# Four slots of weights at four addresses: shifting the rings of a two-layer decoder trunk

## The chip, the cores and the metric

The kernel runs on one core of a Trainium2 chip. The metric is the device time of one execution in microseconds, as the median of several runs; a profile records one execution instruction by instruction, and its times count from the start of its span.

## The reference, cut to what matters

16 learned tokens are put ahead of 256 input tokens (272 in all, width 1024), and two layers follow. Everything is float32.

```python
for l in range(2):
    h = h + 0.5 * rmsnorm(swiglu(rmsnorm(h), ffn_w_in[l, 0], ffn_w_out[l, 0]))
    hn = rmsnorm(h)
    u_pool, q, k, v, gate_pool, gate_attn = split(hn @ w_in[l])      # 1024 x 4096 weights
    y_pool = pool_mixer(u_pool) @ w_pool_proj[l]                      # windows 2, 4, 8, 16
    y_attn = sliding_window_attention(q, k, v, sinks[l]) @ w_attn_proj[l]
    merged = sigmoid(gate_pool) * y_pool + sigmoid(gate_attn) * y_attn
    h = h + rmsnorm(merged @ w_o[l])
    h = h + 0.5 * rmsnorm(swiglu(rmsnorm(h), ffn_w_in[l, 1], ffn_w_out[l, 1]))
return h[:, 16:]
```

`swiglu(x)` is `(silu(x @ w_gate) * (x @ w_up)) @ w_out` with an inner width of 2816.

## The kernel before

Activations are kept with the width in the partitions and the 272 tokens along the columns: eight k rows of 128 for x, 22 for the inner width (hid). Each float32 product is made from three products in the float32r format: the weights are split into a high part (the value rounded to float32r) and a low part (what is left), and so are the activations. `products` (L561 to L565) issues high weights by high x (L563), high weights by low x (L564) and low weights by high x (L565), all into one PSUM bank.

Weights come in units of 256 output columns. A unit of layer l has a number u from 0 to 103, and lies in slot `u % RING` of three rings with RING = 4 slots each: `raw` as it comes from HBM, `w_hi` and `w_lo`. A slot holds KD * UW = 8 * 256 float32 values, 8192 bytes in each partition. SyncE's queue loads a unit into `raw` once the low split of the unit four before it is done; ScalarE makes the high part (L1027) once TensorE has used the slot; VectorE makes the low part from raw and high part (L1347); TensorE waits on `lo_done` and then uses the unit, two tiles of 128 output columns, eight k rows each (`unit`, `unit_tile`). In such a product a block of 128 weight columns is the stationary operand, which a load puts into the array, and the rows of x or hid stream past as the moving operand. In some places two or three units are open at once, and TensorE goes through all their tiles for one k row before it takes the next (`deep_three`, `deep_pair`). In the last FFN output of layer 1 (`end_out`, L815 to L835) the roles are turned round: 128 tokens of hid are stationary, and 512 columns of a weight slot stream (L826 to L828).

Layer 1 leaves out the 16 learned tokens where it can: its products then take 256 columns, from column 16 on. SwiGLU's gate and up go to VectorE (L1535, L1543), ScalarE (silu) and GpSimd (L1968 to L1973); the norms are sums of squares by ScalarE, VectorE, GpSimd and TensorE.

Addresses are the subject of the change. The allocator puts tensors one behind the other in each partition, at multiples of 32 bytes. `raw` begins at byte 16,512, so `raw`, `w_hi` and `w_lo` all begin at 128 modulo 256 (16,512, 49,280 and 82,048), and `h` at 114,816, which is 128 as well. A filler `to_start` puts `x_hi` at START = 64 modulo LINE = 256; the rows of x and hid are padded to a multiple of 256 bytes, so that each k row begins at 64 too. X_SHIFT moves x within its row in layer 1: by 40 and 44 elements (160 and 176 bytes) for the high and low part in three of its four stages, to 224 and 240, and with the first 16 columns left out (64 bytes) to 32 and 48. The rows of o are 1120 bytes long, so its eight k rows begin at eight different places modulo 256.

Of the kernel before, what the change touches and what calls it, by code (L numbers as in the profile page):

```python
# [27 lines left out]
F32R = mybir.dt.float32r  # L28
# [5 lines left out]
P = 128  # L34
# [15 lines left out]
KD = D // P  # L50
KF = FF // P
UW = 2 * P
RING = 4
# [17 lines left out]
ROW = -(-T * 4 // LINE) * LINE // 4  # L71
X_SHIFT = (((0, 0),) * 4, ((0, 0), (40, 44), (40, 44), (40, 44)))
HID_SHIFT = (((0, 0), (0, 0)), ((0, 0), (0, 0)))
O_ROW, Z_ROW = T + 8, T + 4
O_SHIFT = 4

# [100 lines left out]
def trunk(nc, x_columns, norm_columns, norm_g, ffn_w_in, ffn_w_out, w_in, pool_w_grp, w_pool_proj,  # L177
          sinks, w_attn_proj, w_o, geometry, out):
    with ExitStack() as ctx:
        def sb(name, shape, dt=F32):  # L180
            return ctx.enter_context(nc.sbuf_tensor(name, shape, dt))
# [3 lines left out]


        raw = sb("raw", [P, RING, KD * UW])
        w_hi = sb("w_hi", [P, RING, KD * UW], F32R)
        w_lo = sb("w_lo", [P, RING, KD * UW], F32R)
        h = sb("h", [P, KD, T])  # L190
        sb("to_start", [P, ((START - nc.sbuf_base) % LINE + LINE) // 4])
        x_hi_rows = sb("x_hi", [P, KD, ROW], F32R)
# [227 lines left out]
        def hid_of(l, f):  # L420

            return [rows[:, :, at:at + T] for rows, at in zip((hid_hi_rows, hid_lo_rows), HID_SHIFT[l][f])]

# [1674 lines left out]
```

## Time and profile before

| | |
|---|---|
| median of 3 runs | 1173.44 us (1171.82 to 1173.93) |
| the profiled execution | 1172.02 us |
| its span, first to last instruction | 1170.2 us |
| granted TensorE clock | 0.998 of full |
| read from HBM | 195.4 MB |

TensorE's matmul records overlap: one begins before the one ahead of it has ended, so a mean duration of 288 ns is no distance between two matmuls. That distance is read from the start times in the timeline. PE stands for matmuls, PEld for the loads of stationary blocks, DVE for VectorE, ACT for ScalarE, POOL for GpSimd. L563 is line 563 of the kernel.

### The profile page before, as it was taken

How to read it: one execution, taken by the hardware profiler on the slowest of the kernel's cores; microseconds unless marked ns; L12 is line 12 of the kernel's file. 1: busy time of each engine (PE TensorE's matmuls, PEld its weight loads, DVE VectorE, ACT ScalarE, POOL GpSimd, SP SyncE). 2: the span in 40 equal slices, each digit the busy share in tenths (PEclk: the TensorE clock that was granted, in tenths of full speed). 3: DMA queues.
4: the chain of work that ended last, by engine and by line, in shares of the span. 5: the costliest groups of instructions: out<-in, count | busy, mean ns of one | idle time of the engine just before them, and what ended most of it. 6: DMA issues, size and time to landing. Idle time of an engine off the chain costs nothing.

```text
span 1170.2 us, 23880 instructions
## 1 busy us (share of the span) xinstructions
PE 1160.6 (99%) x9269; PEld 1133.2 (97%) x9269; DVE 734.0 (63%) x1145; ACT 554.6 (47%) x818; POOL 430.2 (37%) x486
## 2 busy tenths in 40 slices
PE   9999999999999999999999999999999999999997
PEld 8999999999999999999999999999999999999986
DVE  7655546968566865544586555459676668755542
ACT  7433335637554643333554333355376546543441
POOL 1945500007211286541109645000073122965500
PEclk9999999999999999999999999999999999999999
DMA  8854458372365365535646553573733753654540
GB/s 289 265 180 157 148 176 235 116 233 80 91 178 183 109 207 182 176 122 182 210 131 203 185 165 125 189 227 118 251 92 91 197 164 121 221 198 161 192 168 36
DMA packets 197934, 197.58 MB, mean 169 GB/s; under 512 B 4448, under 2 KB 191200, under 8 KB 197856
## 3 DMA queue, kind: packets, MB, share of 16 engines
q1 hardware_dynamic: 197712, 196.44, 53.3%
q8 instruction: 55, 0.90, 0.3%
q14 instruction: 23, 0.19, 0.1%
q10 hardware_dynamic: 144, 0.05, 0.0%
HBM read 195.43 MB, written 1.05 MB: 168 GB/s over the span
## 4 chain that ended last, share of the span: by engine, by line
PE 92%; issue 3%; DVE 2%; ACT 1%; DMA 0%; POOL 0%; SPq 0%; DVEq 0%; ACTq 0%; POOLq 0%
PE bank L563 27%; PE bank L565 27%; PE bank L564 27%; PE bank L826 2%; PE bank L828 2%; PE bank L827 2%; DVE w_lo L1347 1%; PE bank L915 1%; PE bank L910 1%; PE bank L869 1%; PE bank L599 1%; PE bank L598 1%; PE bank L880 1%; PE bank L626 0%; PE bank L872 0%
## 5 line engine op out<-in xcount | busy, mean ns | idle before, releaser
L563 PE MATMUL bank<-x_hi,w_hi 128*128 128x272 f32 (+1 forms) x1991 | 573.3, 288 | 0.8 <-DVE w_lo L1756 0.7
L565 PE MATMUL bank<-x_hi,w_lo 128*128 128x272 f32 (+1 forms) x1991 | 567.4, 285 | 0.0
L564 PE MATMUL bank<-x_lo,w_hi 128*128 128x272 f32 (+1 forms) x1991 | 566.3, 284 | 0.0
L1027 ACT ACTIVATE w_hi<-raw 128x2048 fp32r<-128x2048 f32 (+3 forms) x201 | 339.1, 1693 | 403.1 <-PE bank L565 383.5
L1347 DVE TENSOR_TENSOR w_lo<-raw,w_hi 128x2048 fp32r<-128x2048 f32 (+3 forms) x203 | 421.4, 2081 | 142.5 <-ACT w_hi L1027 142.2
L563 PEld LDWEIGHTS bank<-x_hi,w_hi 128*128 128x128 f32 x1991 | 374.9, 188 | 2.0 <-issue 1.2
L564 PEld LDWEIGHTS bank<-x_lo,w_hi 128*128 128x128 f32 x1991 | 375.6, 189 | 0.3
L565 PEld LDWEIGHTS bank<-x_hi,w_lo 128*128 128x128 f32 x1991 | 374.9, 188 | 0.0
L1968 POOL TENSOR_TENSOR hid_hi<-silu,up_r 128x272 f32 x88 | 142.1, 1615 | 149.3 <-DVE up_r L1543 143.2
L565 PE MATMUL bank<-hid_hi,w_lo 128*128 128x272 f32 x528 | 151.3, 287 | 0.0
L563 PE MATMUL bank<-hid_hi,w_hi 128*128 128x272 f32 x528 | 151.3, 287 | 0.0
L564 PE MATMUL bank<-hid_lo,w_hi 128*128 128x272 f32 x528 | 151.3, 286 | 0.0
L1543 DVE TENSOR_TENSOR up_r<-bank,r 128x272 f32<-128x272 f32 x88 | 38.3, 439 | 103.6 <-PE bank L565 86.5
L563 PEld LDWEIGHTS bank<-hid_hi,w_hi 128*128 128x128 f32 x528 | 99.5, 188 | 0.0
L564 PEld LDWEIGHTS bank<-hid_lo,w_hi 128*128 128x128 f32 x528 | 99.5, 188 | 0.0
L565 PEld LDWEIGHTS bank<-hid_hi,w_lo 128*128 128x128 f32 x528 | 99.5, 188 | 0.0
L1973 POOL TENSOR_TENSOR hid_lo<-hid_f,hid_hi 128x272 f32 x88 | 87.7, 997 | 20.0 <-POOL hid_f L1970 20.0
L1535 DVE TENSOR_TENSOR gate_r<-bank,r 128x272 f32<-128x272 f32 x85 | 36.5, 438 | 88.0 <-PE bank L565 87.7
L1970 POOL TENSOR_TENSOR hid_f<-silu,up_r 128x272 f32<-128x272 f32 x88 | 84.3, 958 | 0.0
L1957 POOL TENSOR_TENSOR rt<-var,half 128x3 f32<-128x3 f32 x6 | 6.1, 1015 | 159.4 <-DVE var L1393 159.4
L1953 POOL TENSOR_TENSOR acc<-acc,sq 128x272 f32<-128x272 f32 x20 | 22.8, 1139 | 95.5 <-ACT sq L1037 94.4
L2004 POOL TENSOR_TENSOR acc<-s,stats 128x16 f32<-128x16 f32 x64 | 19.0, 296 | 88.0 <-DVE stats L1696 87.7
(219 smaller groups left out, 1323.4 us busy)
## 6 DMA issues: line engine op xcount, KB each, us to landing
raw<-in_ffn_w_in SPq DMA_DIRECT2D x84, 1024.0 KB, 5.1
raw<-in_w_in SPq DMA_DIRECT2D x24, 1024.0 KB, 5.6
raw<-in_ffn_w_out SPq DMA_DIRECT2D x24, 768.0 KB, 4.2
raw<-in_ffn_w_out SPq DMA_DIRECT2D x24, 640.0 KB, 3.9
raw<-in_ffn_w_out SPq DMA_DIRECT2D x10, 1024.0 KB, 5.0
raw<-in_w_in SPq DMA_DIRECT2D x16, 512.0 KB, 5.4
raw<-in_w_attn_proj SPq DMA_DIRECT2D x32, 256.0 KB, 4.5
raw<-in_w_o SPq DMA_DIRECT2D x8, 1024.0 KB, 5.5
```

What stands on the lines that cost most here:

```text
L563: pe.matmul(ps[:, t0:T], w[0], a_hi[:, t0:T], start=start, stop=False)
L564: pe.matmul(ps[:, t0:T], w[0], a_lo[:, t0:T], start=False, stop=False)
L565: return pe.matmul(ps[:, t0:T], w[1], a_hi[:, t0:T], start=False, stop=stop)
L826: pe.matmul(ps[:, :], hid_hi[:, k, cols], w[0], start=k == 0, stop=False)
L827: pe.matmul(ps[:, :], hid_hi[:, k, cols], w[1], start=False, stop=False)
L1027: last = act.activation(hi, w, ACT.Copy)
L1347: last = dve.tensor_tensor(lo, w, hi.bitcast(F32), ALU.subtract)
L1535: dve.tensor_tensor(gate_r[:, j, :], bank[4 * (unit // 2 % 2) + j if banks is None else banks[j]][:, 0:T], r[:, :], ALU.mult).then_inc(til ...
L1543: dve.tensor_tensor(up_r[:, j, :], bank[banks[j]][:, 0:T], r[:, :], ALU.mult).then_inc(tile_read, 1)
L1968: pool.tensor_tensor(hid_hi[:, ds(i * 2 + j, 1), :].rearrange("p o t -> p (o t)"), silu[:, j, :], up_r[:, j, :], ALU.mult).then_inc(hid_hi ...
L1970: pool.tensor_tensor(hid_f[:, j, :], silu[:, j, :], up_r[:, j, :], ALU.mult).then_inc(hf_ready, 1)
L1973: pool.tensor_tensor(hid_lo[:, ds(i * 2 + j, 1), :].rearrange("p o t -> p (o t)"), hid_f[:, j, :], hid_hi[:, ds(i * 2 + j, 1), :].rearrang ...
```

## The change

The ring of high weights is allocated with 8 more elements (32 bytes) in each slot, the ring of low weights with 16 more (64 bytes). Everything that uses them sees a view of the first 2048 elements of each slot, as before.

```diff
@@ -71,6 +71,7 @@
 ROW = -(-T * 4 // LINE) * LINE // 4
 X_SHIFT = (((0, 0),) * 4, ((0, 0), (40, 44), (40, 44), (40, 44)))
 HID_SHIFT = (((0, 0), (0, 0)), ((0, 0), (0, 0)))
+HI_STEP, LO_STEP = 8, 16
 O_ROW, Z_ROW = T + 8, T + 4
 O_SHIFT = 4
 
@@ -185,8 +186,8 @@
 
 
         raw = sb("raw", [P, RING, KD * UW])
-        w_hi = sb("w_hi", [P, RING, KD * UW], F32R)
-        w_lo = sb("w_lo", [P, RING, KD * UW], F32R)
+        w_hi = sb("w_hi", [P, RING, KD * UW + HI_STEP], F32R)[:, :, 0:KD * UW]
+        w_lo = sb("w_lo", [P, RING, KD * UW + LO_STEP], F32R)[:, :, 0:KD * UW]
         h = sb("h", [P, KD, T])
         sb("to_start", [P, ((START - nc.sbuf_base) % LINE + LINE) // 4])
         x_hi_rows = sb("x_hi", [P, KD, ROW], F32R)
```

## Rows read from the trace of the kernel before

**Rows 1.** The page's table of engines: busy us (share of the span), instructions.
```profile
PE 1160.6 (99%) x9269; PEld 1133.2 (97%) x9269; DVE 734.0 (63%) x1145; ACT 554.6 (47%) x818; POOL 430.2 (37%) x486
```

**Rows 2.** The waits of TensorE, the longest: us in total, times, longest.
```profile
PE bank L1004 <- DVE r L1339: 1.2, 1, 1.2
```

**Rows 3.** Groups of matmuls by shape: count, busy us, mean ns.
```profile
L563 PE MATMUL bank<-x_hi,w_hi 128*128 128x272 f32 x1401 | 405.0, 289 | 0.8 <-DVE w_lo L1756 0.7
L563 PE MATMUL bank<-x_hi,w_hi 128*128 128x256 f32 x590 | 168.3, 285 | 0.0
L563 PE MATMUL bank<-hid_hi,w_hi 128*128 128x272 f32 x528 | 151.3, 287 | 0.0
L826 PE MATMUL bank<-w_hi,hid_hi 128*128 128x512 f32 x88 | 34.6, 394 | 0.0
```

**Rows 4.** Timeline of layer 0, first FFN: start us, duration us, instruction.
```profile
59.73 0.28 PE L563 MATMUL bank<-x_hi,w_hi 128*128 128x272 f32 x1
...
60.22 0.28 PE L564 MATMUL bank<-x_lo,w_hi 128*128 128x272 f32 x1
60.22 0.19 PEld L565 LDWEIGHTS bank<-x_hi,w_lo 128*128 128x128 f32 x1
...
66.39 0.28 PE L563 MATMUL bank<-x_hi,w_hi 128*128 128x272 f32 x1
```

**Rows 5.** Busy by stretch: PE, PEld, DVE, ACT, POOL, granted clock, DMA.
```profile
50.00:60.00 10.00, 10.00 (x84) 10.00 (x83) 5.85 (x5) 3.67 (x4) 9.12 (x8) 1.00 0.51 156
160.00:170.00 10.00, 10.00 (x84) 10.00 (x83) 4.81 (x3) 3.03 (x3) 0.00 (x0) 1.00 0.58 187
```

**Rows 6.** Timeline: o in layer 0, shifted x in layer 1, 53 starts apart.
```profile
344.81 0.29 PE L565 MATMUL bank<-o_hi,w_lo 128*128 128x272 f32 x1
...
351.44 0.29 PE L564 MATMUL bank<-o_lo,w_hi 128*128 128x272 f32 x1
...
832.75 0.29 PE L564 MATMUL bank<-x_lo,w_hi 128*128 128x272 f32 x1
...
839.40 0.29 PE L563 MATMUL bank<-x_hi,w_hi 128*128 128x272 f32 x1
```

**Rows 7.** Last product: timeline, 52 starts apart; durations ns min/median/max of L828.
```profile
1129.63 0.39 PE L828 MATMUL bank<-w_hi,hid_lo 128*128 128x512 f32 x1
...
1141.41 0.39 PE L826 MATMUL bank<-w_hi,hid_hi 128*128 128x512 f32 x1
...
L828 PE MATMUL bank<-w_hi,hid_lo x88: 388/389/398, 1102.5 to 1163.6; 128*128 128x512 f32 x88
```

**Rows 8.** Loads beside short matmuls in the timeline; durations ns min/median/max.
```profile
207.02 0.19 PEld L599 LDWEIGHTS bank<-x_hi,w_lo 128*128 128x128 f32 x1
...
207.46 0.19 PEld L599 LDWEIGHTS bank<-x_hi,w_lo 128*128 128x128 f32 x1
...
L563 PEld LDWEIGHTS bank<-x_hi,w_hi x1991: 186/188/193, 5.8 to 1101.6; 128*128 128x128 f32 x200
L564 PEld LDWEIGHTS bank<-hid_lo,w_hi x528: 187/188/189, 137.8 to 791.2; 128*128 128x128 f32 x176
```

**Rows 9.** Timeline, 256 columns: ordinary units (57 starts), two units in turn (56).
```profile
951.79 0.28 PE L564 MATMUL bank<-x_lo,w_hi 128*128 128x256 f32 x1
...
958.45 0.28 PE L563 MATMUL bank<-x_hi,w_hi 128*128 128x256 f32 x1
...
1009.73 0.28 PE L565 MATMUL bank<-x_hi,w_lo 128*128 128x256 f32 x1
...
1016.45 0.28 PE L565 MATMUL bank<-x_hi,w_lo 128*128 128x256 f32 x1
```

**Rows 10.** Splits of a full slot by shape: count, busy us, mean ns, idle before.
```profile
L1027 ACT ACTIVATE w_hi<-raw 128x2048 fp32r<-128x2048 f32 x131 | 250.7, 1916 | 269.7 <-PE bank L565 250.3 <-PE bank L828 9.8 <-DMA raw<-in_ffn_w_in 9.3
L1347 DVE TENSOR_TENSOR w_lo<-raw,w_hi 128x2048 fp32r<-128x2048 f32 x133 | 315.8, 2376 | 47.7 <-ACT w_hi L1027 47.5
```

**Rows 11.** The chain that ended last, in order of time: one of its six splits.
```profile
387.49 2.44 DVE w_lo L1347
```

## The prediction, made before the changed kernel ran

> **What bounds the kernel now.** I began with the table of engines: TensorE is busy for 1160.6 of the 1170.2 us, VectorE for 734.0 and ScalarE for 554.6 [rows 1]. The list of waits then says how little TensorE waits for the engines that fill the two rings: 1.2 us for anything at the longest [rows 2], and 0.7 us for a low split [rows 3]. So the time is, to within one per cent, the sum of the distances between the starts of consecutive matmuls. The groups by shape give the counts: products with 272 columns on x and on hid (1401 + 528 per line, three lines, so 5787), 590 per line on x with 256 columns (1770), and 88 per line with 512 columns, where the weights are the moving operand (264) [rows 3]. Their "mean ns of one" is no pace, since matmuls overlap; the pace comes from start times in the timeline. In the first layer 54 starts take 66.39 - 59.73 = 6.66 us, 123.3 ns each [rows 4]; on hid, from 160 to 170 us, as many matmuls fall into 10 us as on x [rows 5]. 272 columns at the granted clock (full, that is 2.4 GHz [rows 5]) are 113.3 ns, so each product carries 10.0 ns more. The change can act on the time almost only through those 10 ns.
>
> **What the change does to addresses.** A slot holds 8192 bytes, a multiple of 256. All four slots of both rings therefore start at byte 128 modulo 256 today, and so does every 128-column block in them (they lie 512 bytes apart). Afterwards the high slots start at 128, 160, 192, 224. The ring of low weights is moved on by the 128 bytes that the high ring gained, so its slots start at 0, 64, 128, 192: slot 0 of the low weights changes too, and only slot 0 of the high ones and slot 2 of the low ones keep their place. h moves from 128 to 0; x_hi and all that lies after it moves by exactly 256, because the filler ahead of x_hi rounds it off. raw stays. No instruction, wait, transfer or byte moved is added or removed. The change does what its description says, so that is no rival here.
>
> **Step 1, the moving operand.** That a start address can set the pace is in this trace. In layer 1 the copy of x is shifted, so that with all 272 columns its high and low parts start at 224 and 240; 53 starts then take 839.40 - 832.75 = 6.65 us, 125.47 ns each, 2.14 ns above the 123.33 at 64 [rows 6]. The o operand, whose eight k rows start at eight residues, runs at (351.44 - 344.81) / 53 = 125.1 ns [rows 6]. These are changes of the moving operand with the weights always at 128. The change moves it in one place: the last output product, where the weights stream. It now runs at (1141.41 - 1129.63) / 52 = 226.5 ns for 512 columns [rows 7]. Its price is between 264 x -4 ns = -1.1 us and 264 x 9 ns = +2.4 us: 4 ns is about twice the 2.14 ns of a 272-column product, for twice the columns; 9 ns is the longest duration of one of its lines above the median, 398 against 389 [rows 7]. I take 4 ns for half the slots, 132 x 4 = +0.5 us.
>
> **Step 2, the stationary operand.** This is where nearly all uses of the two rings lie, and the trace has only one residue of it. What speaks for no effect: the load of the next block starts together with the matmul before it (both at 60.22), and where matmuls are short, loads follow each other at (207.46 - 207.02) / 4 = 110 ns [rows 4, 8]. Against 123.3 ns that leaves a load 13 ns of room in every product, and its own duration hardly moves: 187 to 189 ns on all 528 of a line on hid, 186 to 193 on x [rows 8]. A load that takes a few ns more from 160 than from 128 has that room. What speaks against: in layer 1 the same shifted x with 256 columns runs at (1016.45 - 1009.73) / 57 = 117.9 ns in ordinary units, and at (958.45 - 951.79) / 56 = 118.9 where two units take turns on one k [rows 9]. All residues are the same in both; what differs is the order of weight blocks and banks. So something beside the moving operand's start enters. The two bounds for this step are those of the rivals below, -14 and +14 us; I take 0, since the nearest row, the load on hid, shows neither a wait nor a stretched load.
> The page "TensorE: Matmul & The Clock Gate" of the Trainium skill, Part 2, says that TensorE reads its two operands through two independent ports, so that a load takes nothing from the running matmul. By that rule step 2 is 0. The same page, Part 1, gives a warm pace of columns / 2.4 GHz plus about 2.5 ns, that would be 115.8 ns; the trace disagrees with 123.3. By its figure, as an estimate, 7.5 ns on each of 5787 products (43 us) is a cost that the page has no reason for, and a reader who believes that it is a clash of operands would expect this change to move it. No term of my sum uses it.
>
> **Step 3, writers and readers.** The four slots may have been meant to keep ScalarE's and VectorE's writes away from TensorE's reads. There is nothing to gain: in two stretches of 10 us, with GpSimd idle or busy for 9.12 us, ScalarE for 3.03 or 3.67 and VectorE for 4.81 or 5.85, as many matmuls (84) fall into each [rows 5]. Price 0. The splits themselves, 1916 ns on ScalarE and 2376 ns on VectorE for a full slot [rows 10], are hidden behind TensorE, for which the high splits of full slots waited 250.3 us. Cover is missing in one place per layer: three low splits, up to 2.44 us long, lie on the chain that ended last in layer 0, in the normalisation before the second FFN, and three in layer 1 [rows 11]. Should the new starts change a split by a tenth (0.24 us), six of them are 1.4 us either way; VectorE's reads of h at residue 0 are in the same bound. I take 0. The transfers into raw wait for the low split and land in unchanged slots: 0.
>
> **The sum.** 1170.2 + 0.5 + 0 + 0 = 1170.7 us of span; the profiled execution took 1172.0, so 1.8 us lie around the span, and the median of the three runs, 1173.4, is 1.4 above that execution. 1170.7 + 1.8 + 1.4 = 1173.9; forecast 1174 us. A measurement of this kernel can tell some 0.2% (2.3 us) from no change.
>
> **Rival 1, slower: loads and streams fall out of step.** Suppose the pace depends on the distance between the moving start and the weight block. Then 64 against 128 is today's pair for 5691 products (5787 less the 96 at 224/240), and it has the lowest excess that the trace shows for any pair: 10.0 ns, against 12.1 at 224/240 and 11.8 on o [rows 4, 6]. The change takes the high weights of slots 1 and 3 to another distance by an odd multiple of 32 bytes. If those slots run like the shifted x, half of 5787 products pay 2.14 ns, 6.2 us; half of 1770 pay the 1.0 ns between the two paces with 256 columns [rows 9], 0.9 us; with the 0.5 of step 1 that is 7.6 us, so 1181. If all four slots pay, since the low ones move as well, it is 12.4 + 1.8 + 0.5 = 14.7, so 1188. It decides from a mean pace above 123.8 ns in layer 0 (0.4 ns x 5787 = 2.3 us). For it: the shifted x and the two paces with 256 columns [rows 6, 9]. Against: the unstretched loads and their 13 ns of room.
>
> **Rival 2, faster: the new distances fit better.** By the same mechanism, but today's pair isn't the best one. Half the slots gaining as much as the shifted x loses give -6.2 - 0.9 us, so 1166 to 1167; all slots, and every product at 121.2 ns, give about 1160. Ten ns of excess leave room for it, and no row has a lower one for 272 columns, which is against it. With 256 columns the present excess is 11.2 ns (117.9 - 106.7), above the 10.0 at 272, so there at least a better distance exists.
>
> **How the numbers follow.** No effect through the loads, 0.38, 1174 (1172 to 1175.5 with the bounds of steps 1 and 3). Rival 1, 0.35, 1177 to 1188, most of it about 1181. Rival 2, 0.27, 1160 to 1170, most of it about 1167. Both signs hold much of the chance, since step 2 has no row of its own: the trace shows one residue. For 8 in 10 I leave out the case of all slots on both sides: 1164 to 1185. The likeliest case alone has 1172 to 1176. Chances: faster 0.27, same 0.38, slower 0.35.
>
> **What would show each step.** The pace in the first layer's FFN, start to start over one unit of each slot: 123.3 in all four if step 2 holds. A pattern that repeats every fourth unit, with slots 1 and 3 off, is the distance between the operands; a pace that is off by the same in all units would point at something else. The last product: 226.5 ns in the slots at 128, more in the others if step 1 holds. Durations of loads (188 ns) above 193 would say that a load is stretched. The mean of the full splits, 1916 and 2376 ns, tests step 3. The prediction is wrong if any slot shows another pace on x or hid.

## The result, and the profile after

The changed kernel takes 1185.49 us (median of 4 runs, 1185.28 to 1185.72) against 1172.8 us (4 runs, 1171.82 to 1173.93) of the kernel before, run beside it. The ratio is 1.0107, with a 95% interval of 1.0095 to 1.0118: slower by some 1%, about 13 us. The profiled execution took 1185.55 us with a span of 1183.8 us; the span is 13.6 us longer than that of before. The granted clock is 0.998 in both.

The kernel after, the page's table of engines (busy us, share of the span, instructions), answers to [rows 1]:

```profile
PE 1174.6 (99%) x9269; PEld 1146.0 (97%) x9269; DVE 731.7 (62%) x1145; ACT 555.3 (47%) x818; POOL 429.4 (36%) x486
```

Every count of instructions is the same. TensorE is busy for 14.0 us more, VectorE for 2.3 us less, ScalarE for 0.7 more. The list of TensorE's waits (us in total, times, longest) answers to [rows 2], and hasn't changed:

```profile
PE bank L1005 <- DVE r L1340: 1.2, 1, 1.2
...
PE bank L564 <- DVE w_lo L1757: 0.6, 1, 0.6
```

So no engine makes TensorE wait longer; its matmuls themselves stand further apart. (Every line of the kernel has moved by one: L564 to L566 are the three products here, L827 to L829 those of the last output.) The timeline shows it best. These are the first matmuls of five units in a row in layer 0's first FFN, in slots 0, 1, 2, 3 and 0 again, 48 matmuls from one to the next (start us, duration us, instruction):

```profile
79.86 0.28 PE L564 MATMUL bank<-x_hi,w_hi 128*128 128x272 f32 x1
...
85.89 0.28 PE L564 MATMUL bank<-x_hi,w_hi 128*128 128x272 f32 x1
...
91.87 0.29 PE L564 MATMUL bank<-x_hi,w_hi 128*128 128x272 f32 x1
...
97.91 0.29 PE L564 MATMUL bank<-x_hi,w_hi 128*128 128x272 f32 x1
...
103.99 0.28 PE L564 MATMUL bank<-x_hi,w_hi 128*128 128x272 f32 x1
```

The units take 6.03, 5.98, 6.04 and 6.08 us, which divided by 48 is 125.6, 124.6, 125.8 and 126.7 ns a matmul. Before, it was 123.3 in every slot [rows 4]. No slot kept its pace, and the four differ. From here on "the pace of a slot" is this number; read from two starts given to 0.01 us, it can be off by 0.1 to 0.2 ns. In the changed kernel the means over all such units of layer 0's first FFN are 125.6, 124.5, 125.9 and 126.6, and each slot repeats its own in layer 0's second FFN and in layer 1's first. The last product answers to [rows 7]: two starts 52 matmuls apart lie 12.07 us apart, 232.1 ns each, against 226.5 before.

```profile
1144.72 0.39 PE L827 MATMUL bank<-w_hi,hid_hi 128*128 128x512 f32 x1
...
1156.79 0.40 PE L828 MATMUL bank<-w_lo,hid_hi 128*128 128x512 f32 x1
```

Adding up the distances between consecutive starts in the whole trace, kind by kind, gives the account of the 13.6 us. Distances above 150 ns (250 ns with 512 columns), where TensorE turns to other work or waits, aren't in the rows of the table, so the counts lie a little below those of the instructions:

| products | count | ns before | ns after | us |
|---|---|---|---|---|
| x, 272 columns | 4157 | 123.48 | 125.65 | +9.0 |
| hid, 272 columns | 1584 | 123.34 | 125.70 | +3.7 |
| last output, 512 columns | 259 | 227.36 | 232.21 | +1.3 |
| x, 256 columns | 1742 | 118.07 | 117.97 | -0.2 |

All that is left, the long distances included, changes by -0.2 us together.

Loads, writers and readers hardly moved (VectorE's split is 22 ns shorter). The durations of the loads (ns, shortest/median/longest) answer to [rows 8], and the two splits (count, busy us, mean ns, idle before) to [rows 10]:

```profile
L565 PEld LDWEIGHTS bank<-hid_lo,w_hi x528: 187/188/189, 140.1 to 803.7; 128*128 128x128 f32 x176
L564 PEld LDWEIGHTS bank<-x_hi,w_hi x1991: 186/188/193, 5.8 to 1113.9; 128*128 128x128 f32 x200
```

```profile
L1028 ACT ACTIVATE w_hi<-raw 128x2048 fp32r<-128x2048 f32 x131 | 251.1, 1919 | 275.3 <-PE bank L566 260.3 <-PE bank L829 10.2 <-DMA raw<-in_ffn_w_in 4.4
...
L1348 DVE TENSOR_TENSOR w_lo<-raw,w_hi 128x2048 fp32r<-128x2048 f32 x133 | 312.9, 2354 | 50.5 <-ACT w_hi L1028 50.4
```

A load is recorded with some 188 ns from the new addresses too, and yet the products that use the loaded blocks stand further apart. That is the reading to take from this pair of views: a duration of a load that hasn't changed doesn't say that the pair of load and matmul costs the same.

### The profile page after: what moved, and what is told of

The parts are those of the page before. It is cut to its first block, busy times and chain, and to the rows that moved or that the text cites. A ratio compares the mean times of both kernels' runs of the same rounds, so it can differ in the third digit from the quotient of the medians.

```text
span 1183.8 us, 23880 instructions
## 1 busy us (share of the span) xinstructions
PE 1174.6 (99%) x9269; PEld 1146.0 (97%) x9269; DVE 731.7 (62%) x1145; ACT 555.3 (47%) x818; POOL 429.4 (36%) x486
## 4 chain that ended last, share of the span: by engine, by line
PE 97%; DVE 1%; ACT 0%; DMA 0%; SPq 0%; issue 0%; POOL 0%; DVEq 0%; ACTq 0%
PE bank L564 28%; PE bank L566 28%; PE bank L565 28%; PE bank L827 2%; PE bank L829 2%; PE bank L828 2%; PE bank L916 1%; PE bank L911 1%; PE bank L715 1%; PE bank L599 1%; PE bank L600 1%; PE bank L627 1%; PE bank L870 1%; DVE w_lo L1348 1%; PE bank L881 0%; PE bank L873 0%
## 5 line engine op out<-in xcount | busy, mean ns | idle before, releaser
L564 PE MATMUL bank<-x_hi,w_hi 128*128 128x272 f32 (+1 forms) x1991 | 573.9, 288 | 0.8 <-DVE w_lo L1757 0.6
L566 PE MATMUL bank<-x_hi,w_lo 128*128 128x272 f32 (+1 forms) x1991 | 569.7, 286 | 0.0
L564 PEld LDWEIGHTS bank<-x_hi,w_hi 128*128 128x128 f32 x1991 | 374.8, 188 | 2.0 <-issue 1.2
L566 PEld LDWEIGHTS bank<-x_hi,w_lo 128*128 128x128 f32 x1991 | 374.6, 188 | 0.0
L566 PE MATMUL bank<-hid_hi,w_lo 128*128 128x272 f32 x528 | 152.1, 288 | 0.0
L564 PE MATMUL bank<-hid_hi,w_hi 128*128 128x272 f32 x528 | 152.0, 288 | 0.0
L564 PEld LDWEIGHTS bank<-hid_hi,w_hi 128*128 128x128 f32 x528 | 99.3, 188 | 0.0
L566 PEld LDWEIGHTS bank<-hid_hi,w_lo 128*128 128x128 f32 x528 | 99.3, 188 | 0.0
```

Source lines behind the costliest of these rows:

```text
L564: pe.matmul(ps[:, t0:T], w[0], a_hi[:, t0:T], start=start, stop=False)
L566: return pe.matmul(ps[:, t0:T], w[1], a_hi[:, t0:T], start=False, stop=stop)
```

## The experiments

Every kernel here is the one before with the edit shown, and all compute the whole result. A kernel with a single time below ran once, so differences of 1 to 3 us between two such times say nothing; the verdicts rest on the pace by slot in the 272-column units, read over 48 matmuls at a time. Within one FFN it repeats within 0.3 ns from unit to unit of a slot, with three exceptions: slot 1 of experiment 8 runs at 125.1 to 126.6, slot 1 of experiment 6 once at 124.4 instead of 126.7, and slot 1 of the changed kernel once at 125.0 instead of 124.5. In experiments 2, 3 and 6 to 10 the filler ahead of x_hi is also shortened or taken out to make room; x_hi begins at START modulo 256 all the same. All places are bytes modulo 256. "Distance" is the start of x less the start of the weight block. In the kernel before, high and low weights lie at 128 and x and hid at 64: distance 192 everywhere.

**1. All slots alike, the low ring on its own.** The change does two things: it makes slots differ, and it moves the two rings against each other. This kernel does the second alone.

```diff
+        sb("pad_lo", [P, 32])
         w_lo = sb("w_lo", [P, RING, KD * UW], F32R)
+        sb("pad_h", [P, 32])
         h = sb("h", [P, KD, T])
```

> No slot is moved against another: only the whole ring of low weights lies 128 bytes further on, so that all high slots begin at 128 and all low slots at 0 modulo 256, as in slot 0 of the changed kernel. h stays at 128. Theory A (the pace of a product is set by where the stationary blocks lie, whether by their distance to the moving operand or by their own place): every unit of layer 0 runs at the 125.6 ns of slot 0 in the changed kernel, against 123.33 before; 5787 x 2.3 ns = 13 us, so about 1186 us. Theory B (the slots differ from each other, and so a split that writes one slot while TensorE reads another meets it differently): the slots do not differ here, so 123.3 ns and 1173 us.

Measured: 1183.41 us (4 runs, 1183.06 to 1184.68) against 1172.41, ratio 1.0091 (1.0074 to 1.0108). The timeline, first matmuls of two units in slot 0, four units (192 matmuls) apart:

```profile
79.65 0.29 PE L565 MATMUL bank<-x_hi,w_hi 128*128 128x272 f32 x1
...
103.69 0.29 PE L565 MATMUL bank<-x_hi,w_hi 128*128 128x272 f32 x1
```

24.04 us / 192 = 125.2 ns, the same in all four slots (in layer 0's second FFN it is 125.5, again in all four). No slot differs from another and most of the loss is there, 11.0 us. So differing slots aren't needed for the loss, nor is another place of h, which lies at 128 again; with the low ring moved on by 128 bytes, the stationary block of one matmul in three is elsewhere, and that is enough.

**2. Both rings in steps of 64 bytes, always alike.** If it were enough that high and low weights of a slot lie at the same place, this kernel would keep its time. Slots lie at 128, 192, 0 and 64.

```diff
+HI_STEP, LO_STEP = 16, 16
...
-        w_hi = sb("w_hi", [P, RING, KD * UW], F32R)
-        w_lo = sb("w_lo", [P, RING, KD * UW], F32R)
+        w_hi = sb("w_hi", [P, RING, KD * UW + HI_STEP], F32R)[:, :, 0:KD * UW]
+        w_lo = sb("w_lo", [P, RING, KD * UW + LO_STEP], F32R)[:, :, 0:KD * UW]
```

> Both rings with slots 64 bytes further apart, so that the high and the low part of a unit begin at the same place: 128, 192, 0 and 64 modulo 256 in slots 0 to 3; x and hid at 64. Theory A1 (distance between moving operand and stationary block): slot 0 at 123.33 ns, the others at other paces, 124 to 127. Theory A2 (high and low block must lie alike, since a triple of products goes from one to the other): 123.33 ns in all four slots, since they lie alike everywhere, and 1173 us. Theory A3 (own place of the block): as A1 here, told apart by the next kernel.

Measured: 1184.47 us. The same five unit starts:

```profile
80.22 0.29 PE L564 MATMUL bank<-x_hi,w_hi 128*128 128x272 f32 x1
...
86.15 0.29 PE L564 MATMUL bank<-x_hi,w_hi 128*128 128x272 f32 x1
...
92.23 0.29 PE L564 MATMUL bank<-x_hi,w_hi 128*128 128x272 f32 x1
...
98.31 0.29 PE L564 MATMUL bank<-x_hi,w_hi 128*128 128x272 f32 x1
...
104.33 0.29 PE L564 MATMUL bank<-x_hi,w_hi 128*128 128x272 f32 x1
```

5.93, 6.08, 6.08 and 6.02 us: 123.5, 126.7, 126.7 and 125.4 ns. Slot 0, which kept its place, kept its pace; the others lost 2 to 3.4 ns. To be alike isn't enough.

**3. The same rings, x and hid moved by 64 as well.** This tells a bad weight address from a bad distance.

```diff
-LINE, START = 256, 64
+LINE, START = 256, 128
```

> The same rings as in the kernel with both steps at 64 bytes (128, 192, 0, 64 modulo 256), but x and hid begin at 128 modulo 256 and no longer at 64. Theory A1 (distance between moving operand and stationary block, modulo 256): the paces of the four slots move on by one slot: slot 1 (192 against 128) now has the 123.33 ns that slot 0 (128 against 64) had, and slot 0 has that of slot 3 there. Theory A3 (own place of the stationary block): the same pace in the same slot as there, slot 0 at 123.33 ns. Neither: the paces depend on both addresses for themselves, and match nowhere.

Measured: 1184.45 us.

```profile
79.76 0.29 PE L563 MATMUL bank<-x_hi,w_hi 128*128 128x272 f32 x1
...
85.78 0.29 PE L563 MATMUL bank<-x_hi,w_hi 128*128 128x272 f32 x1
...
91.71 0.29 PE L563 MATMUL bank<-x_hi,w_hi 128*128 128x272 f32 x1
...
97.79 0.29 PE L563 MATMUL bank<-x_hi,w_hi 128*128 128x272 f32 x1
...
103.87 0.29 PE L563 MATMUL bank<-x_hi,w_hi 128*128 128x272 f32 x1
```

6.02, 5.93, 6.08 and 6.08 us. The pattern of the run before has moved on by exactly one slot, as x did. Slot 1 at 192, slow with x at 64, is now the fast one, and slot 0 at 128, fast in the kernel before, is slow. What counts is the distance. The 256-column units of layer 1 say the same: 118.8, 118.0, 117.4 and 116.7 ns in slots 0 to 3 of experiment 2, and 116.7, 118.8, 118.0 and 117.4 here. That it counts modulo 256 is shown by what stays even: the k rows of x lie 1280 bytes apart and the weight blocks 512, so the true distance takes many values in one unit, and only its rest modulo 256 is the same.

**4. The low ring alone in steps of 64** (low slots at 128, 192, 0, 64; high at 128).

```diff
+HI_STEP, LO_STEP = 0, 16
...
-        w_lo = sb("w_lo", [P, RING, KD * UW], F32R)
+        w_lo = sb("w_lo", [P, RING, KD * UW + LO_STEP], F32R)[:, :, 0:KD * UW]
```

> High slots all at 128; low slots at 128, 192, 0, 64 modulo 256; x and hid at 64, h at 128. Theory A: slot 0 at 123.33 ns (nothing moved), slot 2 at the 125.6 ns of slot 0 in the changed kernel (high 128, low 0), slots 1 and 3 show what the low block alone does at 192 and 64; one product in three loads a low block, so if a product pays for its own block only, the triple of slot 2 pays 3 x 2.3 = 6.9 ns in one place; if the whole triple is out of step, it is spread over all three. Theory B (slots that differ): slot 0 is slower too, since it works beside slots that lie elsewhere.

Measured: 1182.67 us; slots at 123.4, 126.6, 124.4 and 125.5 ns. Slot 0 is again untouched. Slot 2 has the very addresses of experiment 1 (128 and 0 against 64), but runs at 124.4 ns here and at 125.2 there: 0.8 ns that addresses don't explain.

**5. Each load against the block that streams past it meanwhile.** While a matmul runs, the next block is loaded [rows 4]. Perhaps a load minds the stream beside it, not its own. This kernel is experiment 1, with low x and low hid also moved by 128 bytes.

```diff
-X_SHIFT = (((0, 0),) * 4, ((0, 0), (40, 44), (40, 44), (40, 44)))
-HID_SHIFT = (((0, 0), (0, 0)), ((0, 0), (0, 0)))
+X_SHIFT = (((0, 32),) * 4, ((0, 32), (40, 44), (40, 44), (40, 44)))
+HID_SHIFT = (((0, 32), (0, 32)), ((0, 32), (0, 0)))
```

> The low weights at 0 modulo 256 as in the kernel that moved that ring alone (125.2 ns on x and hid), and the low parts of x (layer 0, and the first stage of layer 1) and of hid moved by the same 128 bytes, from 64 to 192; high parts stay (64 and 128). While a product runs, the block of the next one is loaded: beside high x by high weights the high block of the next product, beside low x by high weights the low block, beside high x by low weights the high block of the next k. Theory C (what counts is the distance between the stream that runs and the block that is loaded meanwhile): all three distances are 64 - 128 and 192 - 0 = -64 modulo 256 as before, so 123.3 ns and 1173 us. Theory P (what counts is the distance between the two operands of one product): low x by high weights has 192 - 128 = 64, high x by low weights 64 - 0 = 64, two of three off, so 125 ns or more and 1184 us or more.

Measured: 1184.42 us as the median of 4 runs, which spread from 1180.65 to 1187.37; ratio 1.0089 (1.0065 to 1.0113). Two starts 192 matmuls apart, in the profiled execution, the longest of the four:

```profile
80.43 0.29 PE L565 MATMUL bank<-x_hi,w_hi 128*128 128x272 f32 x1
...
104.75 0.29 PE L565 MATMUL bank<-x_hi,w_hi 128*128 128x272 f32 x1
```

24.32 / 192 = 126.7 ns, worse than experiment 1 and not the 123.3 at which this theory puts it. But this pace isn't that of the whole program. In the same execution, layer 0's second FFN, with every operand at the same places modulo 256, runs otherwise. Two starts there, 192 matmuls apart:

```profile
438.44 0.29 PE L565 MATMUL bank<-x_hi,w_hi 128*128 128x272 f32 x1
...
462.33 0.29 PE L565 MATMUL bank<-x_hi,w_hi 128*128 128x272 f32 x1
```

23.89 / 192 = 124.4 ns, in all four slots and on hid too, while layer 1's first FFN is back at 126.7. Neither pace is 123.3, so the theory falls. One program also differs from itself by 6.7 us here, where the kernel before spreads over 2.9 (1171.87 to 1174.78). A whole FFN of 1584 products at one pace or the other makes 3.5 us (1584 x 2.2 ns), so the four runs may differ in which stages fall into which pace; three of them have no trace, and this isn't shown.

**6 to 8. Both rings alike in steps of 16 bytes**, to read more distances. The slots lie at 96, 112, 128, 144; at 160, 176, 192, 208; and at 32, 48, 64, 80.

```diff
+HI_STEP, LO_STEP = 4, 4
...
+        sb("pad_hi", [P, 56])      # 8 and 40 in the other two
         w_hi = ...                 # and w_lo, as in experiment 2
+        sb("pad_lo", [P, 48])
```

> High and low slots alike at 96, 112, 128, 144 modulo 256, x and hid at 64: the distances moving less stationary are 224, 208, 192, 176 with 272 columns in layer 0, and 192, 176, 160, 144 for high x with 256 columns in layer 1 (16 more for low x). Distance theory: slot 2 at 123.4 ns in layer 0, slot 2 at 117.8 in layer 1; slot 0 and 1 show whether a distance between 192 and 0 is better than 192 (then under 123.3), slot 3 has that of 176. If 192 is a narrow optimum, the other three lie between 124 and 127.

> High and low slots alike at 160, 176, 192, 208 modulo 256: distances 160, 144, 128, 112 in layer 0, and 128, 112, 96, 80 for high x with 256 columns in layer 1. Distance theory: slot 2 has the 126.6 ns that both slots at 128 away had with steps of 64 bytes; the other three show how the pace goes between. No slot is at 123.3 unless the optimum repeats.

> High and low slots alike at 32, 48, 64, 80 modulo 256: distances 32, 16, 0, 240 in layer 0, and 0, 240, 224, 208 for high x with 256 columns in layer 1. Distance theory: slot 2 in layer 0 has the 125.5 ns of distance 0, and slot 2 in layer 1 the 116.7 ns that the slot at 64 had with steps of 64 bytes (distance 224 there for high, 240 for low x), 1.0 ns under what the kernel before has; slots 1 and 3 tell whether 116.7 is the lowest.

Measured: 1186.24, 1184.38 and 1184.55 us. The unit starts of the second:

```profile
80.17 0.29 PE L566 MATMUL bank<-x_hi,w_hi 128*128 128x272 f32 x1
...
86.09 0.29 PE L566 MATMUL bank<-x_hi,w_hi 128*128 128x272 f32 x1
...
92.16 0.29 PE L566 MATMUL bank<-x_hi,w_hi 128*128 128x272 f32 x1
...
98.24 0.29 PE L566 MATMUL bank<-x_hi,w_hi 128*128 128x272 f32 x1
...
104.17 0.29 PE L566 MATMUL bank<-x_hi,w_hi 128*128 128x272 f32 x1
```

Slot 0 (distance 160) takes 5.92 us and slot 3 (distance 112) 5.93, while 144 and 128 between them take 6.07 and 6.08. All distances read so far, both rings alike, 272 columns (at 16 the mean of units from 125.1 to 126.6):

| distance | ns | from |
|---|---|---|
| 192 | 123.3, 123.5, 123.5, 123.4 | before, 2, 3, 6 |
| 160 | 123.3 | 7 |
| 112 | 123.5 | 7 |
| 0 | 125.5, 125.5, 125.4 | 2, 3, 8 |
| 240 | 125.0 | 8 |
| 224 | 125.3 | 6 |
| 16, 32 | 125.9, 125.8 | 8 |
| 64, 128 | 126.6 | 2, 3, 7 |
| 144, 176, 208 | 126.5, 126.6, 126.7 | 7, 6, 6 |

Three distances reach 123.3 to 123.5, none gets below, and between them lie bad ones 16 bytes away. I see no law in the column.

**9. The 256 columns of layer 1.** Several slots of the experiments so far had run below the pace of before there, 117.8 ns. This one goes by slot 3 of experiment 2, 5.60 us for 48 matmuls, 116.7 ns:

```profile
1085.37 0.28 PE L564 MATMUL bank<-x_hi,w_hi 128*128 128x256 f32 x1
...
1090.97 0.28 PE L564 MATMUL bank<-x_hi,w_hi 128*128 128x256 f32 x1
```

This kernel takes its distance over into the kernel before, by moving layer 1's x another 64 bytes on.

```diff
-X_SHIFT = (((0, 0),) * 4, ((0, 0), (40, 44), (40, 44), (40, 44)))
+X_SHIFT = (((0, 0),) * 4, ((0, 0), (56, 60), (56, 60), (56, 60)))
...
+        x_hi_all = sb("x_hi", [P, KD * ROW + 64], F32R)      # x_lo likewise
...
+            return [x[:, at:at + KD * ROW].rearrange("p (k t) -> p k t", t=ROW)[:, :, 0:T]
+                    for x, at in zip((x_hi_all, x_lo_all), X_SHIFT[l][stage])]
```

> The kernel before with one thing changed: in layer 1's three shifted stages x is moved by 56 and 60 elements instead of 40 and 44, so that with 256 columns high and low x begin 224 and 240 bytes beyond the stationary blocks modulo 256, as in the slot at 64 of the kernel with both steps at 64 bytes, which ran at 116.74 ns. Distance theory: 1770 products at 116.74 instead of 117.78 ns are 1.8 us less, about 1171 against 1172.7 us; the pool units of layer 1 (272 columns, now at distances 160 and 176) may go from 125.5 to 123.3 ns, 0.2 us. Rival (the gain of that slot came from its neighbours, since the pace also hangs on the state in which a unit is entered): 117.8 ns or more and no gain.

Measured: 1171.48 us (11 runs, 1170.7 to 1172.29) against 1173.03 (15 runs), ratio 0.9987 (0.9978 to 0.9996). The fastest of all here, if only by 1.5 us, but not by the route expected. Ordinary units still take 5.65 us:

```profile
1057.07 0.28 PE L565 MATMUL bank<-x_hi,w_hi 128*128 128x256 f32 x1
...
1062.72 0.28 PE L565 MATMUL bank<-x_hi,w_hi 128*128 128x256 f32 x1
```

That is 117.7 ns, 117.8 by all units as before, and not 116.7: a distance that is good in one ring isn't in another. What changed is the place where two units take turns on one k, 118.9 before [rows 9]. Two starts 57 matmuls apart now lie 6.71 us apart, 117.7 ns, and where three take turns it is 117.8 instead of 119.2:

```profile
951.74 0.28 PE L566 MATMUL bank<-x_lo,w_hi 128*128 128x256 f32 x1
...
958.45 0.28 PE L566 MATMUL bank<-x_lo,w_hi 128*128 128x256 f32 x1
```

All 256-column distances on x together are 0.8 us shorter than in the trace of before; the rest of the 1.5 us has no account here, and the two profiled executions have nearly the same span (1170.5 and 1170.2 us).

The lowest pace with 256 columns is in experiment 8, in slot 3, which lies at 80 (high x 208 beyond it, low x 224):

```profile
1017.48 0.28 PE L566 MATMUL bank<-x_hi,w_hi 128*128 128x256 f32 x1
...
1023.03 0.28 PE L566 MATMUL bank<-x_hi,w_hi 128*128 128x256 f32 x1
```

5.55 us for 48 matmuls are 115.6 ns (115.7 before rounding), 2.1 below the kernel before. The next unit of the same slot takes 117.9, and so on in turn: 115.7, 117.9, 115.7, 117.9. No kernel was built to keep the better of the two.

**10. Only good distances, but not everywhere the same.** High x at 64 and low x at 32, high weights at 128 and low at 160: the three products of a triple have distances 192 (high, high), 160 (low x, high weights) and 160 (high x, low weights).

```diff
-LINE, START = 256, 64
+LINE, START = 256, 32
-X_SHIFT = (((0, 0),) * 4, ((0, 0), (40, 44), (40, 44), (40, 44)))
-HID_SHIFT = (((0, 0), (0, 0)), ((0, 0), (0, 0)))
+X_SHIFT = (((8, 0),) * 4, ((8, 0), (40, 44), (40, 44), (40, 44)))
+HID_SHIFT = (((8, 0), (8, 0)), ((8, 0), (8, 0)))
...
+        sb("pad_lo", [P, 8])       # ahead of w_lo, and 56 elements ahead of h
```

> Layer 0 only, and the first stage of layer 1: high x and hid begin at 64, low x and hid at 32, high weights at 128, low weights at 160. Two distances between the operands of one product occur, 192 and 160, and both ran at 123.3 ns when all products had them. Theory P (what counts is the distance between the two operands of one product): high by high 64 - 128 = 192, low by high 32 - 128 = 160, high by low 64 - 160 = 160, so 123.3 ns in all slots. Theory C (the stream against the block loaded meanwhile): low x against low block 32 - 160 = 128, the distance that ran at 126.6, so 124.5 to 126.6 ns. Theory T (any change of place from one product to the next puts the triple out of step, which would also explain the 126.67 of the kernel whose low x followed): above 124 ns.

Measured: 1182.04 us; a pace of 124.4 in all slots, from 23.89 us for 192 matmuls:

```profile
79.66 0.29 PE L565 MATMUL bank<-x_hi,w_hi 128*128 128x272 f32 x1
...
103.55 0.29 PE L565 MATMUL bank<-x_hi,w_hi 128*128 128x272 f32 x1
```

Two distances that are each worth 123.3 alone make 124.4 together. So the distance within each pair isn't the whole rule either. (Layer 1's x moves here as well, and its 256 columns run at 120.0 ns, which is some 3 of the 9 us lost.)

**11. The high ring of the change alone** (128, 160, 192, 224), the low ring at 128.

```diff
+HI_STEP, LO_STEP = 8, 0
...
-        w_hi = sb("w_hi", [P, RING, KD * UW], F32R)
+        w_hi = sb("w_hi", [P, RING, KD * UW + HI_STEP], F32R)[:, :, 0:KD * UW]
+        sb("pad_lo", [P, 32])
```

> The part of the change on the high ring alone: high slots at 128, 160, 192, 224, all low slots at 128, x and hid at 64, h at 0 as in the changed kernel. Theory P with the paces of the kernels whose rings lie alike (192: 123.4, 160: 123.3, 128: 126.6, 96 unknown): slot 0 123.3, slot 1 123.3 (160, 160, 192), slot 2 like slot 2 of the changed kernel (125.9, the same addresses), slot 3 125 to 127. Theory T: slot 1 above 124 too.

Measured: 1185.41 us, as much as the whole change. (By the edit h lies at 128 here and not, as expected above, at 0.)

```profile
80.41 0.28 PE L565 MATMUL bank<-x_hi,w_hi 128*128 128x272 f32 x1
...
86.33 0.28 PE L565 MATMUL bank<-x_hi,w_hi 128*128 128x272 f32 x1
...
92.37 0.29 PE L565 MATMUL bank<-x_hi,w_hi 128*128 128x272 f32 x1
...
98.42 0.29 PE L565 MATMUL bank<-x_hi,w_hi 128*128 128x272 f32 x1
...
104.45 0.28 PE L565 MATMUL bank<-x_hi,w_hi 128*128 128x272 f32 x1
```

5.92, 6.04, 6.05 and 6.03 us. Slot 0 has the addresses of before and 123.3 ns. Slot 1 has distances 160, 160 and 192 in its triple, all good ones, and 125.8 ns: the second case against a rule that looks at each pair by itself. The costs don't add up: the high ring's steps alone, and the low ring's move by 128 bytes alone (experiment 1), each cost nearly the whole. In the sums of the traces, the 272-column products lose 10.3 us here, 10.4 in experiment 1 and 12.7 in the changed kernel.

**12. Low x alone.** Rings as before; only low x and low hid are moved, as in experiment 5.

```diff
-X_SHIFT = (((0, 0),) * 4, ((0, 0), (40, 44), (40, 44), (40, 44)))
-HID_SHIFT = (((0, 0), (0, 0)), ((0, 0), (0, 0)))
+X_SHIFT = (((0, 32),) * 4, ((0, 32), (40, 44), (40, 44), (40, 44)))
+HID_SHIFT = (((0, 32), (0, 32)), ((0, 32), (0, 0)))
```

> The rings as in the kernel before (all slots at 128); only the low parts of x (layer 0 and the first stage of layer 1) and of hid move, from 64 to 192, high parts stay at 64. With the kernel that moved only the low weights (125.2 ns) and the one that moved both (126.67) it makes a square. Theory T (any change of place between neighbouring products costs, on either side): above 124 ns, and as the two moves add up to 126.67, about 125 here. Theory W (only the places of the stationary blocks count against each other, and the jump to 126.67 came from the low weights meeting another distance): 123.3 ns.

Measured: 1177.89 us against 1172.54 for the kernel before on the same chip. 23.89 us for 192 matmuls, 124.4 ns in all slots:

```profile
79.14 0.29 PE L563 MATMUL bank<-x_hi,w_hi 128*128 128x272 f32 x1
...
103.03 0.29 PE L563 MATMUL bank<-x_hi,w_hi 128*128 128x272 f32 x1
```

A low x in another place than the high one costs 1.1 ns and a low ring in another place than the high one 1.9 (experiment 1; 2.2 in its second FFN). Both at once cost 3.4 in two FFNs of experiment 5 and 1.1 in the third, so the two don't simply add up.

**What the twelve say together.** This is on the 272-column products where nothing else is said. Shown: the pace depends on the places modulo 256 of the stationary and the moving operand against each other (2, 3). Shown: with any difference of place between high and low, in the rings or in x, no slot runs below 124.4 ns (1, 4, 5, 10, 11, 12, and the change), even where each distance by itself is a good one (10, 11). Refuted: that differing slots as such cost (1, and slot 0 of 4 and 11, which keeps 123.4 beside slots that lie elsewhere), that it is enough to be alike (2), that the load minds the stream beside it and nothing else (5), that each pair counts by itself (10, 11). Open: which part of the chip is fought over, and the rule by which a distance is good. That addresses don't settle the pace alone is shown too: one execution of experiment 5 has 126.7 and 124.4 ns with the same places; 128 and 0 against 64 runs at 125.6 (slot 0 of the change), 125.2 and 125.5 (1) and 124.4 (4); and in layer 1 slot 2 of experiment 6, with weights and x in the places of before modulo 256, takes 120.0 ns where the kernel before takes 117.8. Something beside a unit's own places enters; what went before it is the likeliest, but no run varies that alone. An order of the three products that changes weights less often, or rings and x all at distance 160, would be next; neither was tried.

## Why the prediction was wrong

The forecast was 1174 us in a range of 1164 to 1185; measured are 1185.49, half a microsecond outside, on the side of Rival 1.

- **What bounds the kernel** held: TensorE's pace sets the time, and 12.7 of the 13.6 us of span lie in the 272-column products, where the forecast said they had to lie.
- **Step 2, the stationary operand, is what failed.** Its term was 0, and the products it covers measured +12.5 us (9.0 and 3.7 with 272 columns, -0.2 with 256). I took 0, "since the nearest row, the load on hid, shows neither a wait nor a stretched load". Both observations are still true of the kernel after, 187 to 189 ns and no wait, and it is 1% slower: neither a load's duration nor 13 ns of room between loads measures this cost. It lies in when the next matmul may start, and only the distance of starts shows it. The rows that did bear on it stood in my text, as arguments for Rival 1: another place of x costs 2.14 ns [rows 6], and what differs with the same places is the order of blocks [rows 9]. A cost that depends on the moving operand's place should have been taken to depend on the other's as well until a row spoke against it; no row did.
- The page "TensorE: Matmul & The Clock Gate" of the Trainium skill, Part 2, gives 0 for step 2, since loads and streams read through two ports of their own. For the 272-column products experiment 1 moves nothing but blocks that are loaded, and it adds 1.9 ns to the mean product, so in this kernel the two aren't independent in effect.
- **Rival 1** named the mechanism and its point of decision, a mean pace above 123.8 ns, rightly. Its likeliest case, slots 1 and 3 only, 1181, didn't come: all four slots pay. Slot 0 was taken as safe since its high block keeps its place, but its low block goes from 128 to 0, and experiments 1 and 11 show that such a difference of low and high is a price of its own. Its all-slots case said 12.4 us for the 272 columns; the traces show 9.0 + 3.7 = 12.7. That the pace of the shifted x, 2.14 ns more, gave the size so closely is partly luck: by slot the loss is 1.2 to 3.3 ns, and only the mean of the four is 2.3. Its term for 256 columns, +1.8, was wrong: -0.2.
- **The range** left out exactly this case of all slots on the slow side. Its total, 1188, and the 1181 of the half case had 0.35 between them, and I cut between the two at 1185. With all four slots moved in at least one ring, "half the slots" had no better ground than "all".
- **Step 1, the last product**, had the right sign and bounds (-1.1 to +2.4) but too small a size. A 512-column product pays 4.9 ns by the means of the table (227.4 to 232.2) where I took 4, and the products of every slot pay, not half: +1.3 us instead of +0.5. By unit the means are 230.9 to 233.3, against 226.7 to 229.1 before. Slots at 128 were to keep 226.5; the experiments give no reason why they should, as high and low blocks alternate here too.
- **Step 3, writers and readers**, held: splits at 1919 ns on the full slots (ScalarE) and 2354 (VectorE) against 1916 and 2376, and the longest wait the same 1.2 us. In two stretches with GpSimd busy or idle as many matmuls fall into 10 us again:

```profile
50.00:60.00 10.00, 10.00 (x82) 10.00 (x80) 6.17 (x6) 4.35 (x4) 8.70 (x7) 1.00 0.46 148
160.00:170.00 10.00, 10.00 (x82) 10.00 (x81) 3.76 (x3) 2.94 (x3) 0.00 (x0) 1.00 0.52 165
```

  82 and 82, where it was 84 and 84 [rows 5]: slower by the same on x and on hid, whoever else is busy.
- **A sum that doesn't come out.** The 1172 to 1175.5 given for "no effect through the loads" is narrower than the bounds of steps 1 and 3: 1173.4 with -1.1 to +2.4 and 1.4 either way is 1170.9 to 1177.2. The measured time lies far outside either.
- **Rival 2, faster**, was right in one detail, that 256 columns have a better pace than 117.9 (116.7 in one slot of experiment 2, 115.7 in every second unit of one slot of experiment 8), and wrong for 272, where nothing below 123.3 turned up.

## What to carry to other kernels

Where TensorE is the bound and its matmuls come at a steady distance, the places modulo 256 of weights and activations were worth 1 to 3% of every 272-column product in this kernel. Put the high and the low part of an operand at the same place, at a distance that has been measured as good (to be alike isn't enough, experiment 2), and read the pace of one unit, first start to first start, before and after every edit that moves an allocation. A filler ahead of a tensor or 16 bytes more in each slot is such an edit. Don't judge it by the durations of loads or matmuls or by waits, since none of them moved here. And read it in more than one stage: experiments 1 and 5 have two paces in one execution.

## What the runs showed of the hardware

- The same 272-column product takes 123.3 to 126.7 ns at full granted clock, with loads of 188 ns as before, by where its operands begin modulo 256 and by something more that differs between stages of one execution. With 256 columns on x, units take 115.7 (experiment 8) to 120.0 ns (experiments 6 and 10) a product; with 512 streamed weight columns the means by kernel go from 227.4 (before) to 233.3 (experiment 8).
- Sixteen bytes decide: distance 160 gives 123.3 ns, 144 gives 126.5 and 176 gives 126.6.
- Units fall into repeating cycles. In layer 0's first FFN a triple of products takes 370 ns again and again in the kernel before, 380 in experiment 5, and 376, 371 and 380 in turn in experiment 1. What delays a product by that much stays open.
- The cycle can differ with the same addresses: in experiment 5 it is 380 ns in one FFN and 377 and 370 in turn in the next, and its four runs lie 6.7 us apart.
